# 64 instead of 32 tokens left out of the dense first expert passes of a two-layer PEER decoder

## The chip, the cores and the metric

The kernel runs on one core of one Trainium2 chip. The metric is the device time of one execution in microseconds (us), the median of several runs. The engines are called as in the profile: PE (TensorE, with PEld for its weight loads), DVE (VectorE), ACT (ScalarE), POOL (GpSimd, which here mostly issues indirect DMAs) and SP (SyncE, which issues the weight stream).

## What is computed

Two decoder layers over 256 tokens of width 2048: the first has stick-breaking attention, the second latent attention; each ends with the PEER feed-forward layer, which is the part that matters here. It scores 8 heads x 128 x 128 product keys, picks 16 experts per token and head out of 16384, and sums over them:

```python
s1 = einsum('bshd,hkd->bshk', q[..., 0, :], keys_1); s2 = einsum('bshd,hkd->bshk', q[..., 1, :], keys_2)
v1, i1 = lax.top_k(s1, 16); v2, i2 = lax.top_k(s2, 16)
top_sc, pos = lax.top_k((v1[..., :, None] + v2[..., None, :]).reshape(b, s, 8, 256), 16)
ids = take_along_axis(cand_id, pos); g = softmax(top_sc)
u = take(expert_u, idx)                      # 128 rows of 2048 numbers for every token
act = gelu(einsum('ced,cd->ce', u, hx))
out = einsum('ce,ced->cd', g * act, take(expert_v, idx))
```

## The kernel before

**Two ways to the same activations.** A PEER layer runs in two halves of 128 tiles (`TILES`), one tile being the 128 experts of one first key. The *first passes* multiply all rows of `expert_u` with the normed tokens, whether a token chose the expert or not; the *output passes* multiply `expert_v` with the gated activations, for all 256 tokens. The first passes are not made for all tokens: the last `SPARSE` = 32 of the 256 are left out (`DENSE` = 224 go through PE), and for those 32 only the 128 rows that each token chose are fetched and dotted. Token and expert pairs are laid out over the 128 partitions: one row fetch (`gather`, L602) brings 128 rows of 8 KB, one for each of the 32 tokens times `PAIR_GROUPS` = 4 choices, so a head takes `PER_HEAD` = 4 fetches and a layer `GATHERS` = 32. One dot on DVE (`dot`, L1416) handles one fetch against the normed tokens, which lie in PSUM (`normed_pairs`).

**The tile loop** (`peer`). Each weight is split into a high and a low part in fp32r. For tile j:
- SP streams 1 MB into one of 3 slots `raw`. ACT writes the high halves `hi` (L673), DVE the low halves `lo` (L1099), 1024 columns each, two of each for a tile, two tiles ahead of PE.
- PE (`feature_half`) makes 16 matmuls of `hi` with both parts of the tokens, 2 x `DENSE` = 448 columns wide (L1741), and 16 of `lo`, 224 wide (L1744). It fills one of two banks and needs `a_free` of the tile two before.
- ACT copies the second half of the bank (`copy_part`, L849), DVE adds it to the first (`sum_tile`, L1403, which gives the bank back) and every second tile scales two of them (L1407); ACT takes the GELU of the two (L855) and stores four tiles at a time in DRAM.

**Beside it, by tile number.** DVE does the routing of the heads (`route_step`), four steps a head, the last at tile 80 or so. Dots stand at fixed tiles (`DOTS`): dot j at tile 7j/2, behind that tile's sum and routing step. After a head's last dot come its GELU (`PAIR_GELUS`, L860) and weighting (`PAIR_COEFS`, L1423).

**POOL's list** (`scatter`), in order: 32 slots q, four for each head. A slot has four scatters of gates of the first 128 tokens into `w_rows` (L628), the row fetches of `gathers_in(q)`, the pair scatters of `pair_heads_in(q)` (a head's finished coefficients into `pair_w`, L613, at q = 7, 10, 14, 17, 21, 24, 28 and 31), and three scatters of gates of the other 96 dense tokens (L637; `LATE_COLS` = 12 a head, laid out by `spread_pairs` on ACT). Fetch j waits until dot j - 3 is done, since there are three row buffers (`GATHER_BUFS`). A head's first scatter waits until all of the head before it have landed.

**Where the halves meet.** ACT's `load_group(layer, 0)` at tile 122 waits for every scatter of the layer (`scattered`, `pair_scattered`), and stands in ACT's own queue ahead of the next tiles' work:

```python
if g == 0:
    for h in range(PEER_HEADS):
        act.wait_ge(scattered[h], 16 * (TOPK + LATE_COLS) * (layer + 1))
    act.wait_ge(pair_scattered, 16 * GATHERS * (layer + 1))
```

Then the first four tiles of activations, pair values and gates are loaded, multiplied, split, and the output passes begin. In them each of 128 tiles is 24 matmuls of 512 columns for all 256 tokens.

Of the kernel before, what the change touches and what calls it, by code (L numbers as in the profile page):

```python
# [39 lines left out]
P = 128  # L40
# [9 lines left out]
PEER_HEADS = 8  # L50
# [12 lines left out]
LINE = 512  # L63
STAGED = 2 * GROUP

SPARSE = 32
DENSE = S - SPARSE
FIRST_SPARSE = P - SPARSE
PAIR_GROUPS = P // SPARSE
PER_HEAD = TOPK // PAIR_GROUPS  # L70
GATHERS = PEER_HEADS * PER_HEAD
GATHER_BUFS = 3

LATE_COLS = TOPK * FIRST_SPARSE // P
RANK = 256
# [140 lines left out]
PAIR_COPIES = {step_unit(4 * h + 3) + 2: h for h in range(PEER_HEADS)}  # L216


DOTS = {7 * j // 2: j for j in range(GATHERS)}
PAIR_GELUS = {7 * (PER_HEAD * h + PER_HEAD - 1) // 2 + 1: h for h in range(PEER_HEADS)}  # L220
PAIR_COEFS = {tile + 1: h for tile, h in PAIR_GELUS.items()}


def gathers_in(q):

    return [j for j in range(GATHERS) if 7 * j // 8 == q]


def pair_heads_in(q):
# [18 lines left out]
def build_program(nc, x, x_t, positions, stream, keys, gains, final_g, inv_freq, u_rows0, u_rows1, peer_g, out):  # L248
    with ExitStack() as ctx:
# [35 lines left out]
        def place(name, kb, shape, dt=F32):  # L285
            size = 4 * int(np.prod(shape[1:]))
            assert kb * KB + size <= arena_kb * KB, name
            return nc.alloc_sbuf_tensor_at(name, shape, dt, offset=arena_at + int(kb * KB))
# [54 lines left out]
        place_u = place("place_u", 32, [P, 3, P], U32)  # L343
        gate = place("gate", 33.5, [P, NC_TOK, P])
        pair_u = place("pair_u", 34.5, [P, 2, GATHERS], U32)
        pair_gate = place("pair_gate", 34.75, [P, GATHERS])
        pair_dot = place("pair_dot", 34.875, [P, GATHERS])
        pair_coef = place("pair_coef", 35, [P, GATHERS])
        part = place("part", 36, [P, 2, DENSE])
        late_u = place("late_u", 38, [P, PEER_HEADS * LATE_COLS], U32)  # L350
        late_gate = place("late_gate", 38.5, [P, PEER_HEADS * LATE_COLS])
# [32 lines left out]
        w_dram = [nc.dram_tensor(f"w_rows{k}", (NKEYS, P, DENSE), F32, kind="Internal").ap() for k in range(2)]  # L384
        pair_dram = [nc.dram_tensor(f"pair_w{k}", (P, NKEYS, SPARSE), F32, kind="Internal").ap() for k in range(2)]
        a_dram = [nc.dram_tensor(f"act_rows{k}", (GROUPS, P, GROUP * DENSE), F32, kind="Internal").ap() for k in range(2)]
# [54 lines left out]
        pairs_ready = sem("pairs_ready")  # L441
        gathered = [sem(f"gathered{i}") for i in range(GATHER_BUFS)]
        dots_done = sem("dots_done")
# [50 lines left out]
        def _(sp):  # L494
# [24 lines left out]
            def store_zeros(k, g):  # L519
# [6 lines left out]
                else:  # L526
                    half = NKEYS // 2 * (g - ZERO_ROWS)
                    dst = pair_dram[k][:, half:half + NKEYS // 2, :].rearrange("p (a h) t -> p a (h t)", h=S // SPARSE)
                    src = zeros[k][:].unsqueeze(1).to_broadcast([P, NKEYS // 2 * SPARSE // S, S])
                sp.dma_start(dst, src).then_inc(zeroed[k], 16)  # L530
# [15 lines left out]
        def _(pool):  # L546
# [48 lines left out]
            def gather(layer, j):  # L595

                pool.wait_ge(pairs_ready, layer * PEER_HEADS + j // PER_HEAD + 1)
                if j >= GATHER_BUFS:
                    pool.wait_ge(dots_done, layer * GATHERS + j - GATHER_BUFS + 1)
                elif j == GATHER_BUFS - 1:  # L600
                    pool.wait_ge(normed_in, layer + 1)
                pool.indirect_dma_start(pair_rows[j % GATHER_BUFS][:], None, u_rows[layer],  # L602
                                        bass.IndirectOffsetOnAxis(ap=pair_u[:, 1, j:j + 1], axis=0)).then_inc(
                                            gathered[j % GATHER_BUFS], 16)

# [11 lines left out]
            def scatter(layer):  # L617

                pool.wait_ge(zeroed[layer], 16 * ZERO_STORES)
                rows = w_dram[layer].rearrange("i p t -> (i p t)").unsqueeze(1)  # L620
                for q in range(GATHERS):
                    h, i = divmod(q, PER_HEAD)
                    if i == 0:
                        pool.wait_ge(sel_ready, layer * PEER_HEADS + h + 1)
                        if h >= 1:
                            pool.wait_ge(scattered[h - 1], 16 * (TOPK + LATE_COLS) * (layer + 1))
                    for k in range(TOPK * h + 4 * i, TOPK * h + 4 * i + 4):
                        pool.indirect_dma_start(  # L628
                            rows, bass.IndirectOffsetOnAxis(ap=place_u[:, 0, k:k + 1], axis=0), gate[:, 0, k:k + 1],
                            None, compute_op=ALU.add).then_inc(scattered[h], 16)  # L630
                    for j in gathers_in(q):
                        gather(layer, j)
                    for late in pair_heads_in(q):
                        scatter_pairs(layer, late)
                    pool.wait_ge(pairs_ready, layer * PEER_HEADS + h + 1)
                    for k in range(LATE_COLS * h + 3 * i, LATE_COLS * h + 3 * i + 3):
                        pool.indirect_dma_start(  # L637
                            rows, bass.IndirectOffsetOnAxis(ap=late_u[:, k:k + 1], axis=0), late_gate[:, k:k + 1],
                            None, compute_op=ALU.add).then_inc(scattered[h], 16)
# [449 lines left out]
        def _(dve):  # L1089
# [291 lines left out]
            def peer(layer):  # L1381
# [53 lines left out]
                for j in range(TILES):  # L1435
# [3 lines left out]
                    route_step(layer, 2 * PEER_HEADS + j)  # L1439
                    if j in DOTS:  # L1440
                        dot(DOTS[j])
# [813 lines left out]
```

## Time and profile before

| | |
|---|---|
| median of 3 runs | 3561.59 us (3561.41 to 3561.95) |
| profiled execution: time | 3562.09 us |
| profiled execution: span in the trace | 3560.3 us |
| busy, share of the span | PE 99%, PEld 88%, DVE 62%, ACT 50%, POOL 41% |
| granted TensorE clock | 0.999, full speed (2.4 GHz) |
| DMA | 886.46 MB, mean 249 GB/s |
| layer 0: sum of tile 0 of the first passes | 495 us |
| layer 0: first matmul of the output passes | 1143 us |
| layer 1: the same two | 2205 us, 2853 us |

Times in the rows below are microseconds from the span's start. "Busy" of PE includes matmuls whose ends are modelled, so 99% says that PE hardly pauses, not that it runs at its peak. The shares are means over a program of very different stages: DVE's 62% and POOL's 41% hide that both are far busier in the first passes. A row of the timeline gives start, duration, engine, line, operation, and in brackets the idle time before it with what ended it; "xN" merges N instructions.

### The profile page before, as it was taken

The numbers are of one execution on the slowest core, as the hardware profiler recorded it, in microseconds if no ns is written. First come the engines' busy times: TensorE is split into PE (matmuls) and PEld (weight loads), VectorE is DVE, ScalarE is ACT, GpSimd is POOL, SyncE is SP. The second block draws the span as 40 slices with busy tenths as digits, with TensorE's granted clock in tenths as the row PEclk, the third lists the DMA queues.
The fourth block names the chain that finished last, engine by engine and source line by source line (L and its number), as shares of the span: only waits on it lengthen the run. The fifth ranks groups of instructions, "written<-read, shape, count | busy, mean of one in ns | idle before, by whom it ended". The sixth has DMA issues, their size and how long they took to land.

```text
span 3560.3 us, 48859 instructions
## 1 busy us (share of the span) xinstructions
PE 3536.0 (99%) x19072; PEld 3116.6 (88%) x19072; DVE 2224.3 (62%) x3275; ACT 1763.0 (50%) x2522; POOL 1473.4 (41%) x802
## 2 busy tenths in 40 slices
PE   8999999999999999999999999999999999999998
PEld 7888899999999888888889889999999988888887
DVE  5565588988776444444455548899887654444444
ACT  4355455555545444444455544555554444444443
POOL 2211376778783222222212126777777422222221
PEclk9999999999999999999999999999999999999999
DMA  9844588998988888877754357889899876666664
GB/s 334 295 159 159 203 262 282 277 296 277 297 262 268 277 282 284 280 264 241 238 183 164 117 202 237 289 273 293 281 292 280 252 250 241 241 239 243 236 238 172
DMA packets 327575, 886.46 MB, mean 249 GB/s; under 512 B 123824, under 2 KB 226224, under 8 KB 235440
## 3 DMA queue, kind: packets, MB, share of 16 engines
q1 hardware_dynamic: 132992, 718.38, 56.3%
q0 software_dynamic: 83328, 69.51, 9.7%
q10 hardware_dynamic: 111024, 95.44, 8.5%
q8 instruction: 151, 2.47, 0.3%
q14 instruction: 80, 0.66, 0.1%
HBM read 816.38 MB, written 65.27 MB: 248 GB/s over the span
## 4 chain that ended last, share of the span: by engine, by line
PE 98%; DVE 2%; DMA 0%; ACT 0%; issue 0%; DVEq 0%; SPq 0%; ACTq 0%
PE banks L1741 29%; PE banks L1744 16%; PE banks L1942 13%; PE banks L1946 13%; PE banks L1944 13%; PE banks L1771 3%; PE banks L1773 3%; PE banks L1772 3%; PE banks L1864 0%; DVE lo L1099 0%; PE banks L2112 0%; PE banks L1845 0%; PE banks L1846 0%; PE banks L1847 0%; PE banks L1805 0%; PE banks L2113 0%
## 5 line engine op out<-in xcount | busy, mean ns | idle before, releaser
L1099 DVE TENSOR_TENSOR lo<-raw,hi 128x1024 fp32r<-128x1024 f32 x1077 | 1321.5, 1236 | 929.6 <-ACT hi L673 925.7
L673 ACT ACTIVATE hi<-raw 128x1024 fp32r<-128x1024 f32 x1278 | 1338.4, 1056 | 974.5 <-PE banks L1946 692.7
L573 POOL TENSOR_TENSOR lo<-raw,hi 128x1024 fp32r<-128x1024 f32 x201 | 488.5, 2431 | 1728.6 <-ACT hi L673 1728.5
L1741 PE MATMUL banks<-act_t,hi 128*128 128x448 f32 (+1 forms) x5120 | 1128.6, 372 | 12.9 <-ACT hi L673 9.5
L1741 PEld LDWEIGHTS banks<-act_t,hi 128*128 128x128 f32 x5120 | 938.6, 189 | 111.2 <-issue 9.5
L1744 PEld LDWEIGHTS banks<-act_t,lo 128*128 128x128 f32 x5120 | 631.9, 192 | 13.1
L1744 PE MATMUL banks<-act_t,lo 128*128 128x224 f32 (+1 forms) x5120 | 639.6, 277 | 0.0
L1942 PE MATMUL banks<-hi,wa 128*128 128x512 f32 x2024 | 623.5, 389 | 0.0
L1944 PE MATMUL banks<-lo,wa 128*128 128x512 f32 x2024 | 623.4, 389 | 0.0
L1946 PE MATMUL banks<-hi,wa 128*128 128x512 f32 x2024 | 623.3, 389 | 0.0
L628 POOL DMA_INDIRECT w_rows<-gate,place_u x256 | 457.3, 1786 | 157.7 <-issue 74.8
L1944 PEld LDWEIGHTS banks<-lo,wa 128*128 128x128 f32 x2024 | 380.0, 188 | 78.8
L1946 PEld LDWEIGHTS banks<-hi,wa 128*128 128x128 f32 x2024 | 380.0, 188 | 78.8
L1942 PEld LDWEIGHTS banks<-hi,wa 128*128 128x128 f32 x2024 | 380.0, 188 | 78.6
L849 ACT ACTIVATE part<-banks 128x224 f32<-128x224 f32 x256 | 91.2, 356 | 551.2 <-PE banks L1741 550.9
L637 POOL DMA_INDIRECT w_rows<-late_gate,late_u x192 | 334.5, 1742 | 58.5 <-issue 57.3
L1403 DVE TENSOR_TENSOR stage<-banks,part 128x224 f32<-128x224 f32 x256 | 99.2, 388 | 145.9 <-ACT part L849 145.9
L1416 DVE CUSTOM_DVE_ANT_0 pair_rows<-pair_rows,banks 128x2048 f32<-128x2048 f32 x64 | 145.8, 2279 | 0.0
L613 POOL DMA_INDIRECT pair_w<-pair_coef,pair_u x64 | 109.1, 1705 | 19.5 <-issue 19.5
L602 POOL DMA_INDIRECT pair_rows<-in_u_rows,pair_u x64 | 76.6, 1196 | 78.0 <-DVE pair_dot L1416 60.3
L866 ACT ACTIVATE wa<-acts 128x1024 fp32r<-128x1024 f32 x64 | 67.3, 1052 | 72.8 <-DVE acts L1388 72.8
L1771 PE MATMUL banks<-hi,ot_t 128*128 128x512 f32 x256 | 101.3, 396 | 0.0
(259 smaller groups left out, 2404.7 us busy)
## 6 DMA issues: line engine op xcount, KB each, us to landing
raw<-in_stream SPq DMA_DIRECT2D x647, 1024.0 KB
w_rows<-zeros SPq DMA_DIRECT2D x64, 448.0 KB, 8.1
act_rows<-stage ACTq DMA_DIRECT2D x64, 448.0 KB
acts<-act_rows ACTq DMA_DIRECT2D x64, 448.0 KB, 4.0
w_part<-w_rows ACTq DMA_DIRECT2D x64, 448.0 KB, 5.5
pair_w<-zeros SPq DMA_DIRECT2D x4, 1024.0 KB, 10.1
w_rows<-gate,place_u POOLq DMA_INDIRECT x256, 5.6
acts<-pair_w ACTq DMA_DIRECT2D x64, 64.0 KB, 4.2
```

The source lines that it names most:

```text
L573: pool.tensor_tensor(lo[:, s, :], raw[:, n0 % RAW_SLOTS, j * HALF:(j + 1) * HALF], hi[:, s, :].bitcast(F32), ALU.subtract).then_inc(lo_rea ...
L628: pool.indirect_dma_start(rows, bass.IndirectOffsetOnAxis(ap=place_u[:, 0, k:k + 1], axis=0), gate[:, 0, k:k + 1], None, compute_op=ALU.ad ...
L637: pool.indirect_dma_start(rows, bass.IndirectOffsetOnAxis(ap=late_u[:, k:k + 1], axis=0), late_gate[:, k:k + 1], None, compute_op=ALU.add) ...
L673: act.activation(hi[:, s, :], half, ACT.Copy).then_inc(hi_ready[s], 1)
L1099: dve.tensor_tensor(lo[:, s, :], half, hi[:, s, :].bitcast(F32), ALU.subtract).then_inc(lo_ready[s], 1)
L1416: dve.tensor_tensor_reduce(pair_rows[b][:], pair_rows[b][:], normed_pairs, 1.0, 0.0, ALU.mult, ALU.add, pair_dot[:, j:j + 1]).then_inc(dot ...
L1741: ins = mm(both, hi[:, s, at], act_t[:, kt, :, 0:tokens], start=(kt == 0), stop=(kt == KT - 1), skip_group_check=True)
L1744: ins = mm(ps[:, 0:tokens], lo[:, s, at], act_t[:, kt, 0, 0:tokens], start=False, stop=False, skip_group_check=True)
L1771: mm(o, a_hi, w_hi, start=(kt == 0), stop=False)
L1942: mm(o[:], a_hi, hi[:, s, at], start=first, stop=False)
L1944: mm(o[:], a_hi, lo[:, s, at], start=False, stop=False)
L1946: ins = mm(o[:], a_lo, hi[:, s, at], start=False, stop=last)
```

## The change

`SPARSE` goes from 32 to 64. 64 tokens are left out of the first passes, and the matmuls, sums, scales and GELUs of a tile are 192 (or 384) columns wide instead of 224 (448). `PAIR_GROUPS` becomes 2, `PER_HEAD` 8 and `GATHERS` 64: a layer has 64 row fetches of the same 128 rows each and 64 dots, at tiles 7j/4, and 64 pair scatters, eight a head at the same slots q as before. `LATE_COLS` falls from 12 to 8, so each of POOL's 32 slots has two late scatters instead of three; with the 16 others that makes the 24 scatters a head. The three row buffers stay three. ACT's copies that lay out a head's pairs fall from 16 to 8, the copies of the normed rows between partitions from three DMAs to one. Small tables move to make room. No line of the algorithm changes otherwise.

```diff
-SPARSE = 32
+SPARSE = 64
...
+POOL_SLOTS = 4 * PEER_HEADS
...
-DOTS = {7 * j // 2: j for j in range(GATHERS)}
-PAIR_GELUS = {7 * (PER_HEAD * h + PER_HEAD - 1) // 2 + 1: h for h in range(PEER_HEADS)}
+DOTS = {7 * j // 4: j for j in range(GATHERS)}
+PAIR_GELUS = {7 * (PER_HEAD * h + PER_HEAD - 1) // 4 + 1: h for h in range(PEER_HEADS)}
...
-    return [j for j in range(GATHERS) if 7 * j // 8 == q]
+    return [j for j in range(GATHERS) if 7 * j // 16 == q]
...
-        pair_gate = place("pair_gate", 34.75, [P, GATHERS])
-        pair_dot = place("pair_dot", 34.875, [P, GATHERS])
-        pair_coef = place("pair_coef", 35, [P, GATHERS])
+        pair_gate = place("pair_gate", 35, [P, GATHERS])
+        pair_dot = place("pair_dot", 35.25, [P, GATHERS])
+        pair_coef = place("pair_coef", 35.5, [P, GATHERS])
...
-                for q in range(GATHERS):
-                    h, i = divmod(q, PER_HEAD)
+                for q in range(POOL_SLOTS):
+                    h, i = divmod(q, 4)
...
-                    for k in range(LATE_COLS * h + 3 * i, LATE_COLS * h + 3 * i + 3):
+                    for k in range(LATE_COLS * h + 2 * i, LATE_COLS * h + 2 * i + 2):
```

**POOL, layer 0, slot 7 and the start of slot 8.** `pair_rows_104` to `_106` are the three row buffers. Before:

```order
L628 DMA w_rows<-gate,place_u 3670016x1 x4
L602 DMA pair_rows_106<-in_u_rows,pair_u 128x2048
L602 DMA pair_rows_104<-in_u_rows,pair_u 128x2048
L613 DMA pair_w<-pair_coef,pair_u 524288x1 x4
L637 DMA w_rows<-late_gate,late_u 3670016x1 x3
L628 DMA w_rows<-gate,place_u 3670016x1 x4
L602 DMA pair_rows_105<-in_u_rows,pair_u 128x2048
```

and with the change (lines are one higher there):

```order
L629 DMA w_rows<-gate,place_u 3145728x1 x4
L603 DMA pair_rows_105<-in_u_rows,pair_u 128x2048
L603 DMA pair_rows_106<-in_u_rows,pair_u 128x2048
L603 DMA pair_rows_104<-in_u_rows,pair_u 128x2048
L614 DMA pair_w<-pair_coef,pair_u 1048576x1 x8
L638 DMA w_rows<-late_gate,late_u 3145728x1 x2
L629 DMA w_rows<-gate,place_u 3145728x1 x4
L603 DMA pair_rows_105<-in_u_rows,pair_u 128x2048
```

Between the last fetch of slot 7 and the next fetch there stood 4 + 3 + 4 scatters, and now 8 + 2 + 4. All three buffers are named once before the block of eight, so three fetches are all that the dots have until it is over.

**DVE, layer 0, tiles 1 to 4** of the first passes. Before, the dot after tile 0's is at tile 3:

```order
L1352 RECIPROCAL soft_sum<-soft_sum 128x2
L1354 TENSOR_TENSOR gate<-soft_e,soft_sum 128x2x16
L1099 TENSOR_TENSOR lo<-raw,hi 128x1024
L1403 TENSOR_TENSOR stage<-banks,part 128x224
L1099 TENSOR_TENSOR lo<-raw,hi 128x1024 x2
L1403 TENSOR_TENSOR stage<-banks,part 128x224
L1407 TENSOR_TENSOR stage<-stage,inv_row 128x448
L1099 TENSOR_TENSOR lo<-raw,hi 128x1024
```

With the change a dot stands at tile 1 already, and the next behind tile 3's sum and the routing step that follows these rows:

```order
L1353 RECIPROCAL soft_sum<-soft_sum 128x2
L1355 TENSOR_TENSOR gate<-soft_e,soft_sum 128x2x16
L1417 ISA pair_rows_105,pair_dot<-pair_rows_105,banks 128x2048
L1417 ISA pair_dot 128x1
L1100 TENSOR_TENSOR lo<-raw,hi 128x1024
L1404 TENSOR_TENSOR stage<-banks,part 128x192
L1100 TENSOR_TENSOR lo<-raw,hi 128x1024 x2
L1404 TENSOR_TENSOR stage<-banks,part 128x192
L1408 TENSOR_TENSOR stage<-stage,inv_row 128x384
L1100 TENSOR_TENSOR lo<-raw,hi 128x1024
```

A dot that waits for its rows holds up what is behind it on DVE: the low halves of the next tiles and the sums that give PE's banks back.

## Rows read from the trace of the kernel before

**Rows 1.** Chain that ended last, by engine (page).

```profile
PE 98%; DVE 2%; DMA 0%; ACT 0%; issue 0%; DVEq 0%; SPq 0%; ACTq 0%
```

**Rows 2.** Busy us per stretch: PE, PEld, DVE, ACT, POOL, PEclk, DMA share, GB/s.

```profile
560.00:930.00 370.00, 369.39 (x2352) 349.91 (x2351) 334.18 (x629) 214.17 (x388) 274.57 (x164) 1.00 0.90 289
```

**Rows 3.** Timeline of PE: tiles of 512/256 and 448/224 columns, transposes of 128.

```profile
101.88 3.82 PE L1741 MATMUL banks<-act_t,hi 128*128 128x512 f32 x16
105.53 2.08 PE L1744 MATMUL banks<-act_t,lo 128*128 128x256 f32 x16
107.45 3.82 PE L1741 MATMUL banks<-act_t,hi 128*128 128x512 f32 x16
...
1060.81 3.43 PE L1741 MATMUL banks<-act_t,hi 128*128 128x448 f32 x16
1064.08 1.94 PE L1744 MATMUL banks<-act_t,lo 128*128 128x224 f32 x16
1065.85 3.43 PE L1741 MATMUL banks<-act_t,hi 128*128 128x448 f32 x16
...
2109.78 1.04 PE L1805 MATMUL banks<-ident,x_res 128*128 128x128 f32 x8
2110.57 1.20 PE L1744 MATMUL banks<-act_t,lo 128*128 128x256 f32 x8
```

**Rows 4.** Timeline of DVE, layer 0: sum of tile 0, two dots.

```profile
495.16 0.39 DVE L1403 TENSOR_TENSOR stage<-banks,part 128x224 f32<-128x224 f32 x1 [1.71 <-ACT part L849]
500.96 2.27 DVE L1416 CUSTOM_DVE_ANT_0 pair_rows<-pair_rows,banks 128x2048 f32<-128x2048 f32 x1
...
586.41 2.28 DVE L1416 CUSTOM_DVE_ANT_0 pair_rows<-pair_rows,banks 128x2048 f32<-128x2048 f32 x1
```

**Rows 5.** POOL's groups, 460 to 1105 us: xcount, busy, mean ns, idle before.

```profile
L628 POOL DMA_INDIRECT w_rows<-gate,place_u x128 | 228.3, 1784 | 80.0 <-issue 39.2 <-DMA w_rows<-late_gate,late_u 32.2 <-DVE gate L1354 7.7
L637 POOL DMA_INDIRECT w_rows<-late_gate,late_u x96 | 167.9, 1749 | 29.3 <-issue 28.7 <-DVE pair_dot L1416 0.3 <-ACT late_gate L821 0.3
L613 POOL DMA_INDIRECT pair_w<-pair_coef,pair_u x32 | 53.5, 1671 | 9.8 <-issue 9.8
L602 POOL DMA_INDIRECT pair_rows<-in_u_rows,pair_u x32 | 37.9, 1185 | 39.0 <-DVE pair_dot L1416 30.2 <-issue 8.8
```

**Rows 6.** Timeline of POOL: first and last scatters, three waits, layer 1's last.

```profile
462.10 1.81 POOL L628 DMA_INDIRECT w_rows<-gate,place_u  x1 [7.73 <-DVE gate L1354]
...
467.92 2.49 POOL L628 DMA_INDIRECT w_rows<-gate,place_u  x1 [0.30 <-issue]
...
587.08 1.54 POOL L628 DMA_INDIRECT w_rows<-gate,place_u  x1 [0.30 <-issue]
...
610.73 1.16 POOL L602 DMA_INDIRECT pair_rows<-in_u_rows,pair_u  x1 [15.38 <-DVE pair_dot L1416]
...
752.28 1.16 POOL L602 DMA_INDIRECT pair_rows<-in_u_rows,pair_u  x1 [7.01 <-DVE pair_dot L1416]
...
898.92 1.16 POOL L602 DMA_INDIRECT pair_rows<-in_u_rows,pair_u  x1 [7.77 <-DVE pair_dot L1416]
...
1098.43 1.54 POOL L637 DMA_INDIRECT w_rows<-late_gate,late_u  x1 [0.30 <-issue]
...
2808.18 1.54 POOL L637 DMA_INDIRECT w_rows<-late_gate,late_u  x1 [0.30 <-issue]
```

**Rows 7.** Timeline: ACT's first load of a group in both layers, first output matmul.

```profile
1118.62 0.59 ACTq L789 DMA_DIRECT2D acts<-act_rows  x1
...
2828.36 0.55 ACTq L789 DMA_DIRECT2D acts<-act_rows  x1
...
1143.20 0.63 PE L1942 MATMUL banks<-hi,wa 128*128 128x512 f32 x2
```

**Rows 8.** From issue to landing: of row fetches (L602), of late scatters (L637).

```profile
DMA to landing us min/median/max: 5.5/7.8/11.4
...
DMA to landing us min/median/max: 3.3/5.6/8.5
```

**Rows 9.** DMA, 560 to 930 us: SP's queue (the weight stream), and all packets.

```profile
q1 hardware_dynamic: 10447, 76.15, 56.4%
...
DMA packets 36255, 106.93 MB, mean 289 GB/s; under 512 B 21936, under 2 KB 21936, under 8 KB 24240
```

## The prediction

> **What bounds the kernel now.** The chain of waits first: 98% of it is PE [rows 1], so at a first look only PE's work counts. But the chain shows who was last, not who was nearly last. The stretches show that: from 560 to 930 us, inside layer 0's first passes, PE is busy all the time, DVE for 334 of 370 us, POOL for 275 (and 0.3 us between any two of its instructions is not counted), the DMA engines for 0.90 [rows 2]. Nothing there has much room. Then POOL's groups [rows 5] and its first and last scatter [rows 6]: it starts at 462.1 and is through at 1100.0, 637.9 us later. ACT's `load_group(0)` at tile 122, which waits for these scatters, issues at 1118.6 [rows 7]. The last scatter takes up to 5.6 us from issue to landing [rows 8], so it has landed at about 1104: POOL's list has 15 us of slack before it stops ACT, and with ACT the whole tile loop. Layer 1 is the same: POOL ends at 2809.7, the load is at 2828.4 [rows 6, 7]. So the question is what each of PE, DVE, POOL and DMA needs afterwards.
>
> **PE gets less work.** From the starts in the timeline [rows 3]: 16 passes of 448 columns take 1064.08 - 1060.81 = 3.27 us, 204.4 ns each, and 512 columns 228.1. So 64 columns are 23.7 ns, and 384 come to 180.7 (177.7 if each column is worth 1/2.4 ns). Low passes: 120.0 ns at 256 columns, 110.6 at 224, thus about 101.2 at 192. Bounds: 99, since eight 128-column transposes start 99 ns apart, and 110.6, if it doesn't fall at all. A tile goes from 16 x 315.0 = 5.04 us to 16 x 281.9 = 4.51 (4.43 to 4.66). 256 tiles would give back 136 us. That is what is to be had if nothing else binds. The output passes keep their 256 tokens.
>
> **DVE gets more.** It is busy 334.18 / 370 x 5.04 = 4.55 us a tile where it also routes, to tile 80 or so [rows 2]. The dots go from two in seven tiles to four: 2/7 x 2.28 [rows 4] = +0.65. Sum and scale are narrower by a seventh: at most 0.06 each, of which the scale counts half, -0.1. That makes 5.1 us a tile of pure work against PE's 4.51; with the waits for ACT that can't all vanish I take 5.2. So as far as tile 80 nothing is gained (80 x 0.16 = 13 us lost), and only behind it the tiles could run at 4.51. ACT has less to do throughout; I cost that, the fewer copies between partitions and the moved tables at nothing, since they lie beside busier engines (if they uncovered anything it would be ACT's 214 of 370 us, far from full).
>
> **POOL gets more, and has no room for it.** With the issue gap, one instruction costs [rows 5]: L628 (228.3 + 39.2) / 128 = 2.09 us, L637 2.05, pair scatter L613 1.98, fetch L602 (37.9 + 8.8) / 32 = 1.46. Before: 128, 96, 32 and 32 of them, 574 us, plus 32 for landings at the heads' borders and 30 in three waits for dots: 636, against 637.9 seen. After: 128 x 2.09 + 64 x 2.05 + 64 x 1.98 + 64 x 1.46 = 619 us, +45.
>
> **The waits for dots grow too**, and they need a walk. Fetch j waits for dot j - 3. A dot used to come every 3.5 tiles, so three buffers let POOL run 10 tiles ahead; now it is 5. Slots 0 to 6 have no pair scatters and cost 4 x 2.09 + 2 x 2.05 + 16/7 x 1.46 = 15.8 us each, while their four tiles take 20.8: POOL is held to the tiles' pace. The last fetch of slot 7 is number 18; it waits for dot 15 at tile 26. Tile 0 is summed at 495.2 and its dot starts 5.8 us later [rows 4], so dot 15 ends at 495.2 + 26 x 5.2 + 5.8 + 2.3 = 638. Only from there does POOL run freely. What is left is 46 fetches (67), 96 L628 (201), 50 L637 (103), 64 pair scatters (127) and six borders of 5.4 (32): 529 us. POOL would end at 1167 instead of 1100.
>
> **Two terms that no row shows directly.** First, mutual waits. Each block of eight pair scatters is 16 us, with the six scatters around it 28 us without a fetch, while the three buffered rows last 5 tiles, 27 us, less the 7.8 us that a fetch takes to land [rows 8]. So after a block DVE waits for rows, with PE behind it, and before the next block POOL waits for dots, as it does now for 7.0 and 7.8 us at just that place [rows 6]. Five blocks follow with fetches behind: between 0 and 5 x 7.8 = 39 us; I take half, 20. Second, DMA. The weight stream's 76.15 MB take 56.4% of 370 us, 2.74 us per MB of all 16 engines [rows 9]; the tile's share is 0.90 x 5.04 = 4.54 us now, and 2/7 more of 1.05 MB makes it 5.33: just over DVE's 5.2, so landings lengthen. Between nothing and 3.6 us (7.8 to the longest of now, 11.4) for each of 7 heads, 25 us; I take 7, near the low end, because the excess is only 2%. The Trainium skill speaks more mildly here ("DMA: Bandwidth & Descriptors", Where 436 GB/s comes from): HBM gives one core about 358 GB/s, by which 1.74 MB a tile would be an estimated 4.9 us, no limit, and this term 0. The trace bears out the figure (76.15 MB in 56.4% of 370 us is 365 GB/s), but the other packets take engine time beyond their bytes.
>
> One thing I don't charge: that the dots slow POOL's own instructions. The scatter at 587.08 lies wholly inside a dot and takes 1.54 us, the shortest there is, while others take 2.49 [rows 4, 6]. The skill's "SBUF — State Buffer" (the shared port pair) says that a DVE operation with two SBUF inputs can lock GpSimd out; a reader could fear 32 more dots x 2.3 = 73 us a layer from that. A dot has one input in PSUM, and by that rule as by the row it locks nothing.
>
> **Sum.** POOL ends at 1167 + 20 + 7 = 1194, its last scatter lands 4 us later, ACT loads at 1198 instead of 1118.6: +79. From load to first output matmul it is 24.6 us now [rows 7], mostly five tiles, which are now shorter: -3. So +76 a layer, +153 in all, on the profiled execution's 3562.1 (0.5 above the median, nothing beside this): **3715 us**, 4.3% slower. PE's 136 us don't enter: PE stands still for them and for more.
>
> **Rivals.** A measurement of this kernel can tell about 0.2% (7 us) from no change.
> - *POOL's own list, no mutual waits, DMA free* (15%). For it: the waits may overlap each other. 1167 + 4 = 1171, +52 - 3 = +49 a layer: 3661.
> - *DMA full* (20%). For it: 5.33 us of engine time a tile, and 16 engines that show 0.90 where a tile leaves them room; at 0.90 the tiles to 110 take 5.9 us each, and tile 110, where the last dot stands, comes at 495 + 110 x 5.9 = 1147. Its fetch was issued 10 us before; behind it POOL has slots 28 to 31 and two more, 16 x 2.09 + 10 x 2.05 + 16 x 1.98 + 5 = 91. Load at 1232: +110 a layer, 3783. Against it: nobody waits long for the stream now.
> - *POOL is not the limit* (2%, the other side). Its scatters often take 1.54 us; were all to fall to that with the same 0.3 gap, the work behind fetch 18 would be 210 x 1.84 + 46 x 1.3 + 32 = 478, the end 1116, and the load where it is now. That is the point from which it decides: below 1.84 us a scatter the kernel gets faster. At best tile 122 comes at 495 + 80 x 5.2 + 42 x 4.51 = 1100, -18 - 3 a layer: 3520. Against it: nothing in the change shortens a scatter.
> - That the change doesn't do what it says: the order of instructions shows the new widths and counts, no chance.
>
> **The numbers.** The forecast has 62%, the DMA rival 20, POOL's list alone 15, the last one 2, and 1 is for gains and losses that cancel. The range reaches from a little under POOL's list alone to just past the DMA rival: 3645 to 3790. Faster 0.02, same 0.01, slower 0.97.
>
> **What would show it.** In the new profile: POOL's last scatter near 1194 (under 1171 speaks for its list alone, over 1220 for DMA); ACT's load issued right when it lands; low passes 101 ns apart when PE runs; POOL's waits for dots well over 30 us a layer, some 55 to 100; DVE waiting for `pair_rows`, which it never does now; PE's idle time and chain shares that name DVE, POOL and DMA; output passes as long as before. If POOL ends before 1120 or PE shows no pauses, I am wrong about the limit; if DVE never waits for rows, about the mutual waits.

## The result, and the profile after

| | before | changed |
|---|---|---|
| median of the runs, us | 3561.65 (3561.41 to 3561.95) | 3735.55 (3722.11 to 3741.85) |
| ratio, 95% interval | | 1.0483 (1.0470 to 1.0495) |
| profiled execution, us | 3562.1 | 3722.1 (span 3720.3) |

The changed kernel is 4.8% slower. The forecast was 3715, range 3645 to 3790. Its sum was made against the profiled execution, and there it stands at +153 forecast, +160.0 measured. That execution is the fastest of its four: by the medians the change costs 174 us here, and 167 in a second set of four (the first experiment, median 3729.06). So the forecast is 7 to 21 us too low. The runs of the changed kernel spread over 0.5% in this set and 0.2% in the second, those of the kernel before over 0.02%.

First the page of the changed kernel: busy time of each engine, the granted clock in 40 slices, the software queue (it carries POOL's transfers; 69.51 MB and 9.7% before), and the chain that ended last.

```profile
PE 3479.8 (94%) x19072; PEld 3106.3 (83%) x19072; DVE 2326.9 (63%) x3403; ACT 1739.0 (47%) x2394; POOL 1554.1 (42%) x862
PEclk9999999998998999999999999999988989999999
q0 software_dynamic: 92480, 136.62, 13.5%
PE 61%; POOL 15%; DVE 10%; issue 7%; DMA 6%; ACT 0%; ACTq 0%; DVEq 0%; SPq 0%; POOLq 0%
```

The chain was 98% PE [rows 1] and is 61% PE now; POOL, DVE, DMA and the gaps that the chain calls issue (in the block below, those between POOL's instructions) hold 38%. Over the whole program PE is still busy for 94%, which alone would hide it.

The same line on the page of the kernel before allows a first sum:

```profile
PE 3536.0 (99%) x19072; PEld 3116.6 (88%) x19072; DVE 2224.3 (62%) x3275; ACT 1763.0 (50%) x2522; POOL 1473.4 (41%) x802
```

PE is busy for 56 us less and idle for 216 us more (3720.3 - 3479.8 = 240.5 instead of 3560.3 - 3536.0 = 24.3), which makes the 160. The stretch of [rows 2] shows more (columns: PE, PEld, DVE, ACT, POOL, granted clock, DMA share, GB/s):

```profile
560.00:930.00 370.00, 324.80 (x2144) 317.37 (x2143) 336.70 (x623) 183.63 (x302) 271.16 (x165) 0.94 0.91 309
```

PE makes 2144 matmuls where it made 2352, each on fewer columns, and stands still for 45 us. POOL is busy for 271 of 370 us, no more than before (275): it was near its limit, and its idle time is now landings and dots. POOL's groups of instructions in the changed kernel, from 460 to 1240 us, against [rows 5]:

```profile
L629 POOL DMA_INDIRECT w_rows<-gate,place_u x128 | 230.9, 1804 | 96.6 <-DMA w_rows<-late_gate,late_u 52.5 <-issue 35.4 <-DVE gate L1355 7.5
L614 POOL DMA_INDIRECT pair_w<-pair_coef,pair_u x64 | 115.2, 1800 | 19.5 <-issue 19.5
L638 POOL DMA_INDIRECT w_rows<-late_gate,late_u x64 | 113.2, 1769 | 19.5 <-issue 19.2 <-DVE pair_dot L1417 0.3
L603 POOL DMA_INDIRECT pair_rows<-in_u_rows,pair_u x64 | 72.2, 1128 | 78.9 <-DVE pair_dot L1417 56.0 <-issue 16.2 <-ACT banks L830 6.7
```

Instructions and issue gaps together are (230.9 + 35.4) + (115.2 + 19.5) + (113.2 + 19.2) + (72.2 + 16.2) = 622 us (619 forecast). The view of waits of the changed kernel (us in total, times, longest) shows who stands still for it, in both layers:

```profile
PE banks L1742 <- DVE stage L1404: 218.1, 57, 32.9
ACT hi L674 <- DMA raw<-in_stream: 182.3, 111, 5.5
DVE pair_rows L1417 <- DMA pair_rows<-in_u_rows,pair_u: 119.2, 21, 9.9
POOL w_rows L629 <- DMA w_rows<-late_gate,late_u: 105.0, 14, 11.9
POOL pair_rows L603 <- DVE pair_dot L1417: 98.8, 19, 11.0
ACT stage L856 <- issue: 73.5, 2, 37.7
```

The last line is ACT in front of its load of a group, once a layer. DVE's waits for rows are new. Before, PE waited 2.3 us for DVE's sums and ACT 27.8 us for the weight stream.

**One block of pair scatters.** The timelines of the changed kernel's POOL, DVE and PE show fetch 18, and how a block of eight pair scatters reaches PE. POOL:

```profile
639.39 1.18 POOL L603 DMA_INDIRECT pair_rows<-in_u_rows,pair_u  x1 [10.48 <-DVE pair_dot L1417]
640.87 2.36 POOL L614 DMA_INDIRECT pair_w<-pair_coef,pair_u  x1 [0.30 <-issue]
...
656.47 1.54 POOL L614 DMA_INDIRECT pair_w<-pair_coef,pair_u  x1 [0.30 <-issue]
...
666.31 1.54 POOL L629 DMA_INDIRECT w_rows<-gate,place_u  x1 [4.38 <-DMA w_rows<-late_gate,late_u]
...
673.81 1.00 POOL L603 DMA_INDIRECT pair_rows<-in_u_rows,pair_u  x1 [0.30 <-issue]
```

DVE:

```profile
679.46 2.29 DVE L1417 CUSTOM_DVE_ANT_0 pair_rows<-pair_rows,banks 128x2048 f32<-128x2048 f32 x1 [7.62 <-DMA pair_rows<-in_u_rows,pair_u]
...
682.81 0.35 DVE L1404 TENSOR_TENSOR stage<-banks,part 128x192 f32<-128x192 f32 x1
```

PE:

```profile
683.21 1.01 PE L1742 MATMUL banks<-act_t,hi 128*128 128x384 f32 x2 [9.59 <-DVE stage L1404]
```

POOL waits 10.5 us for dot 15 (the fetch starts at 639.4; 638 was forecast). Then come eight pair scatters, two late ones, the wait for head 1's landings at the border of head 2 (4.4 us) and four others: 34 us from this fetch to the next. The rows run out, DVE stands 7.6 us before its next dot, the sum behind it is late, and PE loses 9.6 us. Both directions of the wait are in one block: POOL for a dot before it, DVE for rows behind it.

**The end of the list.** POOL's last scatter, ACT's load, and PE's restart and first output matmul, of the changed kernel, layer 0, and below them the same ACT row of layer 1; against [rows 6, 7]:

```profile
1198.07 1.54 POOL L638 DMA_INDIRECT w_rows<-late_gate,late_u  x1 [0.30 <-issue]
...
1201.32 0.59 ACTq L790 DMA_DIRECT2D acts<-act_rows  x1
...
1208.10 2.93 PE L1742 MATMUL banks<-act_t,hi 128*128 128x384 f32 x8 [31.04 <-DVE stage L1404]
1210.82 2.60 PE L1745 MATMUL banks<-act_t,lo 128*128 128x192 f32 x16
1213.26 2.97 PE L1742 MATMUL banks<-act_t,hi 128*128 128x384 f32 x16
...
1223.83 0.63 PE L1943 MATMUL banks<-hi,wa 128*128 128x512 f32 x2
...
2991.03 0.55 ACTq L790 DMA_DIRECT2D acts<-act_rows  x1
```

Layer 0's output passes start at 1223.8 instead of 1143.2, +80.6, and this is half of the +160.0. The output matmuls themselves are as before: 389 ns in the groups of both kernels.

### The profile page after: what moved, and what is told of

It is laid out like the page before. It is cut to its first block, busy times and chain, and to the rows that moved or that the text cites. A ratio compares the mean times of both kernels' runs of the same rounds, so it can differ in the third digit from the quotient of the medians.

```text
span 3720.3 us, 48983 instructions
## 1 busy us (share of the span) xinstructions
PE 3479.8 (94%) x19072; PEld 3106.3 (83%) x19072; DVE 2326.9 (63%) x3403; ACT 1739.0 (47%) x2394; POOL 1554.1 (42%) x862
## 4 chain that ended last, share of the span: by engine, by line
PE 61%; POOL 15%; DVE 10%; issue 7%; DMA 6%; ACT 0%; ACTq 0%; DVEq 0%; SPq 0%; POOLq 0%
PE banks L1943 12%; PE banks L1947 12%; PE banks L1945 12%; PE banks L1742 7%; POOL w_rows L629 6%; POOL pair_w L614 5%; DVE lo L1100 4%; PE banks L1745 4%; PE banks L1772 3%; PE banks L1774 3%; PE banks L1773 3%; DMA w_rows<-late_gate,late_u 3%; POOL w_rows L638 2%; DMA pair_rows<-in_u_rows,pair_u 2%; DVE pair_rows L1417 2%
## 5 line engine op out<-in xcount | busy, mean ns | idle before, releaser
L1742 PE MATMUL banks<-act_t,hi 128*128 128x384 f32 (+1 forms) x5120 | 1057.1, 357 | 229.1 <-DVE stage L1404 218.1
L1742 PEld LDWEIGHTS banks<-act_t,hi 128*128 128x128 f32 x5120 | 912.7, 193 | 289.1 <-DVE stage L1404 240.6
L1745 PE MATMUL banks<-act_t,lo 128*128 128x192 f32 (+1 forms) x5120 | 655.0, 281 | 0.0
L1417 DVE CUSTOM_DVE_ANT_0 pair_rows<-pair_rows,banks 128x2048 f32<-128x2048 f32 x128 | 291.9, 2281 | 119.4 <-DMA pair_rows<-in_u_rows,pair_u 119.2
L850 ACT ACTIVATE part<-banks 128x192 f32<-128x192 f32 x256 | 84.1, 329 | 479.2 <-PE banks L1742 478.9
L614 POOL DMA_INDIRECT pair_w<-pair_coef,pair_u x128 | 230.0, 1797 | 39.0 <-issue 39.0
L638 POOL DMA_INDIRECT w_rows<-late_gate,late_u x128 | 225.5, 1762 | 39.0 <-issue 38.7
L603 POOL DMA_INDIRECT pair_rows<-in_u_rows,pair_u x128 | 148.2, 1158 | 160.4 <-DVE pair_dot L1417 98.8
L1404 DVE TENSOR_TENSOR stage<-banks,part 128x192 f32<-128x192 f32 x256 | 90.0, 351 | 40.9 <-ACT part L850 40.6
L856 ACT ACTIVATE stage<-stage 128x384 f32<-128x384 f32 x128 | 65.8, 514 | 92.4 <-issue 73.5
L1772 PE MATMUL banks<-hi,ot_t 128*128 128x512 f32 x256 | 101.2, 395 | 0.0
```

The source lines that it names most:

```text
L614: pool.indirect_dma_start(rows, bass.IndirectOffsetOnAxis(ap=pair_u[:, 0, j:j + 1], axis=0), pair_coef[:, j:j + 1], None, compute_op=ALU.a ...
L638: pool.indirect_dma_start(rows, bass.IndirectOffsetOnAxis(ap=late_u[:, k:k + 1], axis=0), late_gate[:, k:k + 1], None, compute_op=ALU.add) ...
L1417: dve.tensor_tensor_reduce(pair_rows[b][:], pair_rows[b][:], normed_pairs, 1.0, 0.0, ALU.mult, ALU.add, pair_dot[:, j:j + 1]).then_inc(dot ...
L1742: ins = mm(both, hi[:, s, at], act_t[:, kt, :, 0:tokens], start=(kt == 0), stop=(kt == KT - 1), skip_group_check=True)
L1745: ins = mm(ps[:, 0:tokens], lo[:, s, at], act_t[:, kt, 0, 0:tokens], start=False, stop=False, skip_group_check=True)
```

## The experiments

The theory that they test is the forecast's: POOL's list is the limit of the first passes, and it grows by its instructions plus mutual waits between POOL and DVE over three row buffers. Its rivals: DMA is the limit (theory B of the expectations), DVE's work for the dots is it (C), or POOL is not the limit and PE's gain arrives.

**The changed kernel once more**, as the base of the others.

> The changed kernel once more, to have it on the same chip as the variants. All theories: 1.045 to 1.052 of the kernel before, 3720 to 3745 us. What is open is why its executions differ by 0.5% when the kernel before repeats within 0.02%.

3729.06 us (3726.66 to 3733.03), ratio 1.0473 (1.0455 to 1.0490). ACT's first load is at 1201.3 and 2994.9. Differences below are against this median, and waits against this run, unless said otherwise. Waits are sums over both layers where no layer is named.

**The blocks of eight spread** over three slots as 3, 3 and 2; the last head's stays whole.

```diff
-    return [h for h in range(PEER_HEADS) if 7 + 7 * h // 2 == q]
+    return [h for h in range(PEER_HEADS) if 0 <= q - (7 + 7 * h // 2) < 3]
...
-                for j in range(PER_HEAD * h, PER_HEAD * (h + 1)):
+                for j in pairs_of(q, h):
```

> Changed kernel, but the eight pair scatters of a head stand in three slots as 3, 3 and 2 instead of in one (the last head's stay together). POOL's list is as long, the bytes are the same. Theory A (POOL's list plus mutual waits: after a block of eight DVE waits for rows, before the next POOL waits for dots): both waits shrink, 6 to 15 us a layer, so 12 to 30 us under the changed kernel. Theory B (the DMA engines are full): no change. Theory C (DVE's work alone): no change.

3703.49 us (3700.98 to 3706.80): -25.6, as expected. With not an instruction fewer, DVE's waits for rows fall from 121.3 to 95.5 us. It is the order alone that costs these 26 us.

**Rows of half the size**: each fetch brings 4 of 8 KB.

```diff
-                pool.indirect_dma_start(pair_rows[j % GATHER_BUFS][:], None, u_rows[layer],
+                pool.indirect_dma_start(pair_rows[j % GATHER_BUFS][:, 0:D // 2], None,
+                                        u_rows[layer].rearrange("e (a d) -> (e a) d", a=2),
```

> Changed kernel, but each fetch brings 4 KB of a row instead of 8 KB; the dot reads 2048 columns as before, the second half of them stale, so that half of every fetched row is left out of the dots. POOL's instructions and DVE's work are the same (three small memsets a layer added); 0.30 MB a tile less for DMA, back to the bytes of the kernel before. Theory A with DMA as a small term: 15 to 60 us under the changed kernel, POOL ends about 10 to 30 us earlier a layer. Theory B: nearly everything comes back, 110 us or more under. Theory C: no change.

(The index of a row is left as it was and now picks half rows out of twice as many, so the values fetched are others; count and size are what matters here.)

3705.36 us (3700.97 to 3715.23): -23.7. ACT's waits for the weight stream fall from 188.5 to 97.3 us, and the DMA share of 560 to 930 us from 0.90 to 0.83. The load moves by only 2 us in layer 0 (1199.3) and 12 in layer 1, where 10 to 30 a layer were expected; the profiled execution is the slowest of its four (3715.2). Landings do get shorter: fetches land after 6.4 us (median, 8.8 with whole rows), and POOL's waits at the borders fall from 107.5 to 89.1 us, but in layer 0 part of that is taken back by waits for dots (61.6 us instead of 57.2). The bytes of the rows are worth about 24 us; as the limit (B, 110 or more) DMA falls.

**No late scatters**: 64 instructions a layer less for POOL.

```diff
-                    for k in range(LATE_COLS * h + 2 * i, LATE_COLS * h + 2 * i + 2):
+                    for k in ():
```

> Changed kernel without the 64 late scatters a layer (L638 there), so the gates of the second 64 dense tokens stay zero: that part of the result is left out. POOL's list is 131 us shorter a layer, fetches, dots and bytes are as they were. Theory A: 90 to 120 us under the changed kernel, no more, since POOL is then held by the dots and DVE and the tiles' pace remain (POOL would end near 1140 us instead of 1200). Theory B: 0 to 15 us under, as the scatters carry almost no bytes. Theory C: no change.

3599.78 us (3586.71 to 3602.77): -129.3, more than the 90 to 120 expected, and still 38 us over the kernel before (ratio 1.0094, 1.0074 to 1.0115). The view of waits of this kernel shows POOL as the one with time to spare:

```profile
POOL pair_rows L603 <- DVE pair_dot L1417: 324.7, 48, 14.8
```

So the list of POOL was the limit, and 128 scatters less take it away. What is left then is the next limit: in this kernel, from 560 to 930 us DVE is busy for 352.63 of 370 us and the DMA share is 0.94.

**The kernel before with 192 columns** in its first passes, nothing else: what PE's gain is worth with POOL's old list.

```diff
+                            wide = 192 if tokens == DENSE else tokens
-                            ins = mm(ps[:, 0:tokens], lo[:, s, at], act_t[:, kt, 0, 0:tokens], start
+                            ins = mm(ps[:, 0:wide], lo[:, s, at], act_t[:, kt, 0, 0:wide], start
```

(and the same for the high passes).

> The kernel before (32 tokens left out, 32 fetches a layer, POOL's list as it was), with only PE's matmuls of the first passes narrowed to 2 x 192 and 192 columns: the dot products of tokens 192 to 223 are left out, all else is issued as before. It isolates what narrower passes are worth. If PE alone bound the kernel before: 0.47 us x 256 tiles = 120 us under it (3440). Theory A (POOL's list is the next limit, 15 us behind): POOL's waits for dots shrink with faster tiles, but its 574 us of work and the landings stay: 36 to 64 us under the kernel before, 3498 to 3526, with ACT's group load right behind the last landing.

3522.54 us (3518.00 to 3542.02), 39.3 under the kernel before (0.9907, 0.9877 to 0.9938). PE's steady tile is 4.57 us here as in the changed kernel, 0.47 less, which over 256 tiles would be 120 us. Two thirds of that don't arrive, because the load now waits for POOL's list; of this kernel:

```profile
ACT stage L855 <- issue: 54.9, 2, 28.4
```

These were 9.4 us before. The slack that the forecast read from the trace is measured here: in layer 0 the load moves from 1118.6 to 1096.9, 22 us earlier, and then starts 1.8 us behind the end of POOL's last scatter. Five of the 22 come from POOL, which waits less for dots and ends at 1095.2 instead of 1100.0; the other 17 are the slack, forecast as 15. Some 20 us a layer is all that faster tiles can bring.

**The kernel before with each pair scatter issued twice**, the second into an unused tensor: 32 instructions a layer more for POOL, PE and DVE as they were. (Setting the unused tensor to zero adds 2 MB a layer to SP's stores; POOL's first scatter starts at 461.4, as before.)

```diff
+                    pool.indirect_dma_start(
+                        dump[layer].rearrange("p i t -> (p i t)").unsqueeze(1),
+                        bass.IndirectOffsetOnAxis(ap=pair_u[:, 0, j:j + 1], axis=0), pair_coef[:, j:j + 1],
+                        None, compute_op=ALU.add).then_inc(pair_scattered, 16)
```

> The kernel before, with each of its 32 pair scatters a layer issued a second time into an unused tensor: 32 x 1.98 = 63 us more on POOL's list, nearly no bytes, no dots, no rows. Theory A: the slack of 15 us is used up, then every microsecond shows: 38 to 48 us a layer, 76 to 96 us over the kernel before (3638 to 3658). Theories B and C: within 10 us of the kernel before.

3645.56 us (3644.54 to 3647.16): +83.8 to the kernel before (1.0236, 1.0219 to 1.0253), inside the 76 to 96. 32 x 2.0 = 64 us of instructions a layer, less the slack and less some of the old waits for dots (15.4 us in layer 0, 30.2 before), come out as 42 a layer. POOL's list by itself, with no more dots and hardly more bytes, sets the time.

**Dots on 64 of 2048 columns.**

```diff
-                    dve.tensor_tensor_reduce(pair_rows[b][:], pair_rows[b][:], normed_pairs, 1.0
+                    dve.tensor_tensor_reduce(pair_rows[b][:, 0:64], pair_rows[b][:, 0:64], normed_pairs[:, 0:64], 1.0
```

> Changed kernel with dots over 64 columns instead of 2048, so most of each dot is left out; fetches, waits, POOL's list and bytes are the same. DVE has about 2.1 us x 64 = 134 us less a layer. Theory A: DVE's pace in the route part is one partner of the mutual waits, so 40 to 75 us under the changed kernel, and POOL's list still ends last (it can't end before about 1150 us). Theory B: under 10 us. Theory C (DVE alone): 100 us or more under, with POOL done in time.

3670.46 us (3669.77 to 3675.97): -58.6, in the 40 to 75 expected; DVE's work as the limit (C, 100 or more) falls. From 560 to 930 us DVE is busy for only 271.91 of 370 us, and it waits 200.7 us for rows instead of 121.3: it is held by POOL's fetches. DVE's work is a partner in the waits, worth these 59 us, and not the limit by itself.

**Work ahead of the border wait.** A head's fetches and pair scatters go ahead of the wait for the former head's scatters, which they don't need.

```diff
                     if i == 0:
+                        if h >= 1:
+                            fetches()
                         pool.wait_ge(sel_ready, layer * PEER_HEADS + h + 1)
...
-                    for j in gathers_in(q):
-                        gather(layer, j)
-                    for late in pair_heads_in(q):
-                        scatter_pairs(layer, late)
+                    if i or not h:
+                        fetches()
```

> Changed kernel, in which the first slot of each head from the second on issues its fetches and pair scatters ahead of the wait for the last head's landings, so that this wait is filled with work. The waits at the borders are 52 us a layer in the changed kernel. Theory A: if only POOL's list counted, 50 us a layer would come back; since fetches then wait for dots instead, part of it: 16 to 50 us in all under the changed kernel. Theory B: no change.

3683.86 us (3682.07 to 3686.14): -45.2. POOL's waits for landings in layer 0 are 10.8 us (7.2 ahead of scatters, 3.6 ahead of a fetch) instead of 55.0; its waits for dots grow, from 98.4 to 125.2 in both layers. Of the 78 us of landing waits that disappear in both layers (107.5 to 29.3), 45 come out as time.

**Two row buffers instead of three**: the mutual waits by themselves, with every instruction the same.

```diff
-GATHER_BUFS = 3
+GATHER_BUFS = 2
```

> Changed kernel with two row buffers instead of three, so fetch j waits for dot j - 2: the same lists, bytes and work on every engine, only less room between fetches and dots. Theory A with mutual waits: both DVE's waits for rows and POOL's waits for dots grow by 60 us or so, 50 to 65 us a layer, 100 to 130 us over the changed kernel. Were POOL's list alone what counts (no mutual waits): under 25 us. Theory B: no change.

3832.95 us (3825.74 to 3835.99): +103.9, as expected. All three waits grow, from 218.5, 121.3 and 98.4 us; of this kernel:

```profile
PE banks L1742 <- DVE stage L1404: 316.0, 55, 32.9
...
DVE pair_rows L1417 <- DMA pair_rows<-in_u_rows,pair_u: 223.6, 25, 16.6
POOL pair_rows L603 <- DVE pair_dot L1417: 217.1, 33, 22.9
```

**The load two tiles later**, at tile 124.

```diff
-                    if j == TILES - GROUP - 2:
+                    if j == TILES - GROUP:
```

> Changed kernel with ACT's group load at tile 124 instead of 122. POOL ends at the same time; while ACT waits for its scatters PE has two tiles fewer left to do afterwards. Theory A: 7 to 9 us a layer, 12 to 18 us under the changed kernel. If the wait at the load were not on the path: no change.

3721.65 us (3712.95 to 3724.35): -7.4, less than the 12 to 18 expected and as small as the spread of the runs. The first output matmul does follow the load after 16.0 us (22.5 in the first profile of the changed kernel), but in this kernel the load itself is at 1212.6, 11 us later: POOL's waits for landings in layer 0 are 66.0 us instead of 55.0. Why these waits came out longer, with nothing changed ahead of tile 122, is open.

**Spread, border and load together**: all the work of the changed kernel in another order.

> Changed kernel with the three harmless repairs together: pair scatters spread over three slots, fetches ahead of the border wait, group load at tile 124. Alone they are worth 26 and 45 us and an expected 15. Theory A: they overlap a little, 65 to 90 us under the changed kernel, 3640 to 3665, so still 2% or more over the kernel before, since POOL's 619 us of instructions, 45 more than before, and DVE's 5.1 us a tile stay.

3626.34 us (3624.09 to 3629.78): -102.7. That is more than the 65 to 90 expected, and more than the three alone (25.6 + 45.2 + 7.4 = 78.2). The kernel is still 1.8% behind the one before (1.0183, 1.0166 to 1.0200), where "2% or more" was expected. Its stretch from 560 to 930 us, columns as above:

```profile
560.00:930.00 370.00, 341.95 (x2305) 333.98 (x2305) 362.03 (x659) 198.90 (x330) 291.43 (x178) 0.98 0.97 330
```

and its waits:

```profile
ACT hi L686 <- DMA raw<-in_stream: 244.7, 149, 5.5
...
PE banks L1754 <- DVE stage L1416: 132.1, 63, 16.7
POOL pair_rows L610 <- DVE pair_dot L1429: 105.8, 24, 11.0
DVE pair_rows L1429 <- DMA pair_rows<-in_u_rows,pair_u: 49.3, 9, 10.1
```

With POOL's stalls mended, DVE is busy for 98% of the stretch and the DMA share is 0.97. The forecast's reading that "as far as tile 80 nothing is gained" holds even with a better POOL: tile 80 is summed at 915.7 us in this kernel and at 906.5 in the kernel before.

**Everything relieved**: no late scatters, fetches of 2 of 8 KB, dots on 64 columns. PE has the widths of the changed kernel, the other engines hardly any of what it pays for them.

> Changed kernel with everything beside PE relieved at once: no late scatters, fetches of 2 KB instead of 8, dots over 64 columns (those parts of the result are left out). It shows what the narrower passes would be worth with nothing in their way: 0.47 us x 256 tiles = 120 us under the kernel before, 3436 to 3450. If PE had another limit in these passes (its clock, the weight stream), clearly more than 3450.

3463.66 us (3457.86 to 3466.19), 98.5 below the kernel before (0.9726, 0.9709 to 0.9742), where 112 to 126 was expected. Busy times, stretch and waits of this kernel:

```profile
PE 3418.5 (99%) x19072; PEld 3065.7 (89%) x19072; DVE 2078.6 (60%) x3403; ACT 1733.0 (50%) x2394; POOL 1356.6 (39%) x734
...
560.00:930.00 370.00, 368.27 (x2583) 367.26 (x2582) 308.50 (x698) 220.53 (x362) 269.57 (x166) 1.00 0.89 279
```

```profile
POOL pair_rows L603 <- DVE pair_dot L1418: 171.0, 35, 12.7
```

In the stretch PE runs through at full clock, and POOL waits for the dots. PE is busy for 117.5 us less than in the kernel before, close to the 120, but it is idle for 13 us more, which fits ACT's wait in front of the load (21.8 us in both layers, 9.4 before). That leaves 104 us for the profiled execution, the fastest of its four; why the others are up to 8 us slower is open. So PE's gain of 0.47 us a tile is real, and of the kernels tried this is the only one where most of it arrives.

**What PE's clock has to do with it.** This kernel and the changed one have the same matmuls on PE. The changed kernel is busy with them for 3479.8 - 3418.5 = 61 us longer, and its granted clock is 0.969 over the span instead of 0.996. In the changed kernel's trace PE is busy for 103 us while the lower clock level is granted, in this one's for 10. As eight high passes take 2.72 us there (rows of the restart above) and 1.41 at the full level, an estimate of what the lower level costs PE is 50 us and 5: some 45 of the 61. How much of them reaches the time is not shown: where POOL's rows come late, a faster PE would have waited instead. The forecast had no such term.

No version tried beats the kernel before with the whole result. The two that are faster (192 columns in the kernel before, and everything relieved) leave work out.

## Why the prediction was right, step by step

- **The limit** (POOL's list with 15 us of slack): right, by experiment. 64 scatters less a layer give 129 us, 32 more a layer on the kernel before cost 84, and narrower matmuls on the kernel before give 39 instead of 120. The slack is 17 us rather than 15: the forecast charged 4 us for the last landing and called 5.6 us the most that one takes, but 5.6 is the median in [rows 8] and 8.5 the longest, and the last scatter of a layer is waited for much less, as the point on the last landing shows.
- **Start of the free run** at fetch 18: 639.4, forecast 638. It rests on 5.2 us a tile up to tile 26, and they took 5.25 (sums at 494.5 and 631.1 us). A wait for the normed rows (6.7 us, `ACT banks L830` in POOL's groups) was not seen beforehand and left no mark on this start; POOL was held to the tiles' pace there.
- **The free run**, taken as 498 us of instructions, 32 of borders, 20 of waits for dots and 7 for DMA, 557 in all: from 639.4 to 1199.6 it is 560. POOL's groups from 639.3 us on give 500.2 of instructions, 44.8 of landings at the borders (39 with the 7 for DMA), and 15.2 of waits for dots behind fetch 18's own. So landings are 6 us over their term and dots 5 under theirs, and it is luck that they nearly cancel. Within the 500, pair scatters took 8 us more than their 127 (2.10 us each instead of 1.98) and fetches 4 less than their 67.
- **Landings** are the part that was mis-sized. They were kept at 5.4 us a border, with 7 for all lengthening, and came to 44.8 us over the six borders behind fetch 18, 7.5 each; the same six took 29 us in the kernel before. The forecast charged little because it saw the DMA engines only 2% over DVE's pace (5.33 us a tile against 5.2). That excess did not come: 65 tiles are summed from 560 to 930 us, 5.7 us each, and a DMA share of 0.91 makes 5.2 us of engine time for one. Landings lengthened all the same. With half rows the six borders take 36 us, and 47 in the repeat of the changed kernel, so, as far as one execution of each can tell, the bytes of the rows make up 11 of the 18 us or so by which they grew; what makes the rest is open.
- **A published figure for this term.** The Trainium skill ("DMA: Bandwidth & Descriptors", Where 436 GB/s comes from) gives about 358 GB/s from HBM for a core, by which the term would be 0. The trace does not bear out the 0: the stretch moves 309 GB/s, under that figure, and yet landings grew, and ACT's waits for the stream went from 27.8 to 182.3 us over the program. Nor do the 365 GB/s that the forecast set beside the figure show a limit; they are the stream's bytes over the engine time of its own packets. The most that a stretch from 560 to 930 us moved is 330 GB/s, at a share of 0.97 (spread, border and load together).
- **The last landing**, taken as 4 us: ACT's load follows the end of POOL's last scatter after 1.7 us. POOL ended at 1199.6 instead of 1194, the load came at 1201.3 instead of 1198: here, too, two errors partly cancel.
- **From load to output**: 22.5 us instead of 24.6, -2 for the -3 forecast. The narrower tiles take less, but the restart behind the load takes 2 us more than steady tiles.
- **PE's tile**, forecast 4.51 us (4.43 to 4.66), is 4.57. The high pass fell further than thought, to 176.3 ns (180.7), the low pass not at all: rows below. It didn't enter the sum, as the forecast said.
- **The tiles' pace behind fetch 18** was wrong, and did not enter the sum either. The forecast lost 13 us up to tile 80 and let the tiles run at 4.51 us behind it. In fact tile 80 is summed at 941.4 us, 35 later than before (906.5), and tiles 80 to 110, which still carry dots, take 5.7 us each, more than the 5.04 of before. Only behind the last dot do they run at 4.57.
- **Waits on both sides**: DVE's waits for rows appear and the sums behind them are late, as listed. POOL's waits for dots are 56.0 us in layer 0 and 42.8 in layer 1, where 55 to 100 were named; in layer 1 another 11.5 us stand right before a fetch (at 2346.9) without a releaser in the profile.
- **DMA full** (20%): its load at 1232 was not reached. Half rows leave the load within 2 us in layer 0 and give back 24 us in all, where this rival asks for most of the loss.
- **POOL's list alone** (15%): a last scatter under 1171 was its sign; it ended at 1199.6. Two buffers (+103.9) and spread blocks (-25.6) show the mutual waits that it left out. **POOL not the limit** (2%): fell with the result.
- **Not on the list of signs**: the granted clock, 0.969 over the span where it was 0.999, and with it an estimated 50 us of PE's time. Whether a part of that is in the 7 to 21 us that the forecast lacks, no run tells.

The steady tiles of the changed kernel, timeline of PE; against [rows 3]:

```profile
1141.69 1.93 PE L1745 MATMUL banks<-act_t,lo 128*128 128x192 f32 x16
1143.45 2.97 PE L1742 MATMUL banks<-act_t,hi 128*128 128x384 f32 x16
1146.27 1.92 PE L1745 MATMUL banks<-act_t,lo 128*128 128x192 f32 x16
```

The low pass takes (1143.45 - 1141.69) / 16 = 110.0 ns at 192 columns and took 110.6 at 224, so the upper bound of the forecast for the low pass was right, not its middle of 101.2.

## What to carry to other kernels

- An engine that is 41% busy and absent from the chain can still stand some 15 us behind it. Before work moves from the engine on the chain to another one, add up that engine's whole list for the stage, gaps and landings with it, and compare its end with the instruction that waits for it.
- Few buffers between two engines that each work in order turn a burst on one into waits on both: the order of the same instructions was worth 26 us here, one buffer of three 104. Putting independent work ahead of a wait for a landing was worth 45 us.
- Mending the limit shows the next one: 103 us of repairs left the kernel 1.8% behind, with DVE busy for 98% of the route part and a DMA share of 0.97.

## What the runs showed of the hardware that was not expected

- A matmul of 192 columns with weights of its own takes as long as one of 224, 110.0 and 110.6 ns from start to start, also in the kernel before with narrow passes; at 256 columns it is 120.0, at 384 176.3, at 448 204.4. The Trainium skill ("TensorE: Matmul & The Clock Gate", LDWEIGHTS) gives loading 128 columns of weights as P / 1.2, 107 ns. The 110 lie close to that, but the transposes of 128 columns [rows 3] start 99 ns apart, below it, so the figure is no floor for every matmul here. That the weight load is the cause of the 110 was not tested.
- After its pause of 31 us PE starts again at the lower of its two clock levels: the granted clock is 0.50 (1.2 GHz) from 1208.1 to 1210.8 us and 1.00 (2.4 GHz) again from 1213.3 on. In the rows of the restart at 1208.10 eight high passes take 2.72 us, against 2.82 for sixteen in steady tiles, and the 16 low passes behind them 2.44 instead of 1.76. That is 2.0 us more for one restart. A pause of 9.6 us does it too: behind 683.21 eight high passes take 2.73 us, at a granted clock of 0.50. Over the program the lower level costs PE an estimated 50 us of busy time (see the kernel with everything relieved); no run filled the pauses, so what it costs in time is open.
- The changed kernel's runs spread over 0.5% and 0.2% in its two sets, where the kernel before has 0.02 to 0.04%. It is unexplained, and it is not the doing of the mutual waits alone: the kernel before with 192 columns, in which DVE waits 14.0 us for rows and POOL 19.1 for dots, spreads over 0.7%.
